# Joined attention maps transposed by DMA from SBUF to SBUF instead of by way of DRAM

## The chip, the cores and the metric

One Trainium2 chip; the kernel runs as one program on its 8 cores. The metric is the device time of the slowest core, in microseconds (us). Even cores and odd cores have different shares of the work (below), and so different spans.

## The reference, cut to what matters

One decoder block on x (4 x 4096 x 2048) with 16 meta tokens ahead of each sequence. Its input projection feeds two mixers, whose outputs are gated, added, projected and followed by a squared-ReLU MLP. The change lies in the first mixer, differential attention, with 4 heads:

```
s = einsum('bhcqd,bhckd->bhcqk', q, k) * scale      # two maps c = 0, 1
p = softmax(where(kpos <= qpos, s, -inf))           # per map
a = p[:, :, 0] - lam * p[:, :, 1]                   # the joined map
o = einsum('bhqk,bhkd->bhqd', a, v)                 # V has 256 columns
```

The last product contracts over keys, so TensorE needs the joined map with the keys on the partitions: it has to be transposed.

## The kernel before

**Tiling.** A sequence is shared by two cores. The even core ("a" in the tile names) has the first 18 blocks of 128 queries, the odd core ("b") the last 14, and each computes keys and values for all blocks that its queries see (19 on a, with the block of the meta tokens; 33 on b). The phases: 1 makes keys, values and queries; 2 runs attention and retention; 3 the gates and the merge; 4 the output projection; 5 the MLP.

**Phase 2** works on units: one head and one block of 128 queries, 72 units on core a and 56 on core b. Within a head the blocks run downwards in heads 0 and 2 and upwards in heads 1 and 3, so a unit's joined map is 128 x n with n from 256 to 2432 columns on a (2 to 19 blocks of 128 keys) and from 20 to 33 blocks on b. A unit passes through these steps, each a closure that `slot(u)` puts at a fraction of a slot:

- `qk(u, c, g)`: a matmul of up to 512 keys into one of three PSUM banks, then an exponential on ACT (L1284) into `P`. Map 0 goes to `P[u % 2]` (tiles `P_59` and `P_60`), map 1 to `P[2]` (`P_61`).
- `ratio(u)` and `join(u)` (L1308, on DVE), in slot u + 1: the joined map, written in place into `P[u % 2]`.
- `store_a(u)`, at 0.27 of slot u + 1: a DMA of the joined map to DRAM, into `A_d[u % 3]`.
- `load_a(u)`, at 0.62 of slot u + 1: a transposing DMA from `A_d` into `aT[u % LAG]` (tiles `aT_62` to `aT_64` on a); it waits until the store has landed.
- `av(u)`, in slot u + LAG: n / 128 matmuls of `aT` with `V`. LAG is 3 on core a and 2 on core b.

The matmuls of retention (`queue`, `pull`) are spread between these steps, as filling. Between the phases nothing waits for all engines; the first weights of phase 3 (`w_0_2`, `w_0_3` on core a) come in eight pieces each on POOL's DMA queue, each piece waiting for the one before on the same semaphore, and POOL works its stream in order: pieces, small statistics, and the add of `mo` (L1485) of phase 3.

**What sets the order.** Every operation is recorded once (`Prog.op`) with its dependences by buffer. `Prog.schedule` then plays a list schedule with a cost for each operation and writes one stream per engine in the order of that play; at run time each engine works its stream in order and waits on semaphores where a dependence crosses engines. All plain and transposing DMAs here are issued by SP (its queue is shown as SPq, all of its issues at L272, inside `Prog.dma`); loads of weights, which cast to bf16, are issued by POOL. A waiting DMA on SP so holds back all that SP issues behind it. TensorE's matmuls all have line L437, in the helper `mm`; they are told apart by their tiles.

**Buffers that matter.** `P[u % 2]` is read by the joining step and by the store; the exponentials of unit u + 2 overwrite it and so wait for the store's landing. `aT[u % LAG]` is overwritten by the transpose of unit u + LAG, which waits for `av(u)`. The tiles of phase 2 are put by `place`, first fit, into three free stretches of SBUF.

Of the kernel before, what the change touches and what calls it, by code (L numbers as in the profile page):

```python
# [9 lines left out]
BF16 = mybir.dt.bfloat16  # L10
# [363 lines left out]
class Core:  # L374
# [102 lines left out]
    def build(self):  # L477
        nc, p, io = self.nc, self.p, self.io
        self.PSA = io["ps"]
        self.PS = [io["ps"][:, 512 * i:512 * (i + 1)] for i in range(8)]  # L480
        self.PB = [p.buf("ps%d" % i) for i in range(8)]
        T, nch = self.T, self.nch
        self.KT_d = self.dram("KT_d", [4, 128, 2, T], BF16)
        self.V_d = self.dram("V_d", [128, 4, nch, 256], BF16)
        self.xnT_d = [self.dram("xnT%d_d" % i, [128, 16, 128 * n], BF16) for i, (c, n) in enumerate(self.tiles)]
        own = self.own_tiles
        self.QT_d = [self.dram("QT%d_d" % i, [4, 128, 2, 128 * n], BF16) for i, (c, n) in enumerate(own)]
        self.oa_d = self.dram("oa_d", [128 * self.nown, 1024], BF16)
        self.or_d = self.dram("or_d", [128 * self.nown, 1024], BF16)
        self.tT_d = [self.dram("tT%d_d" % i, [128, 16, 128 * n], BF16) for i, (c, n) in enumerate(own)]  # L490
        self.A_d = [self.dram("A%d_d" % i, [128, T], BF16) for i in range(3)]
        self.mT_d = [self.dram("mT%d_d" % i, [128, 16, 128 * n], BF16) for i, (c, n) in enumerate(own)]
        self.hnT_d = [self.dram("hnT%d_d" % i, [128, 16, 128 * n], BF16) for i, (c, n) in enumerate(self.mtiles)]
        self.h1_d = self.dram("h1_d", [self.nown * 128, D], F32)
        NT, NO = len(self.tiles), len(own)
        self.D_KT = [[p.buf("KT_d") for _ in range(NT)] for _ in range(4)]
        self.D_V = [p.buf("V_d") for _ in range(nch)]
        self.D_x = [p.buf("x_d") for _ in range(NT)]
        self.D_Q = [[p.buf("Q_d") for _ in range(NO)] for _ in range(4)]
        self.D_oa = [[p.buf("oa_d") for _ in range(4)] for _ in range(self.nown)]  # L500
        self.D_or = [[p.buf("or_d") for _ in range(4)] for _ in range(self.nown)]
        self.D_tT = [[p.buf("tT_d") for _ in range(2)] for _ in range(NO)]
        self.S_tT = [p.dsem("tT%d" % i) for i in range(2)]
        self.D_A = [p.buf("A_d") for _ in range(3)]
        self.D_m = [[p.buf("m_d") for _ in range(4)] for _ in range(NO)]
        self.D_h1 = [p.buf("h1_d") for _ in range(self.nown)]
        self.D_hn = [p.buf("hn_d") for _ in self.mtiles]

        off = 0
        cst, self.B_cst = self.sb("cst", [128, NCST], F32, off)  # L510
        off += -(-NCST * 4 // 64) * 64
        cstb, self.B_cstb = self.sb("cstb", [128, 256], BF16, off)
        off += 512
        gs4, self.B_gs4 = self.sb("gs4", [128, 256], F32, off)
        off += 1024
        small, self.B_small = self.sb("small", [128, 8], F32, off)
        off += 32
        negh, self.B_negh = self.sb("negh", [128, 4], F32, off)
        off += 32
        self.O = off  # L520
        assert self.base + off + 200 * KB <= self.limit
        self.cst = cst
        self.gs4 = gs4
        self.ident = cstb[:, 0:128]
        self.mask = cstb[:, 128:256]
        self.neglam = small[:, 4:5]
        self.S_c = p.dsem("c")
        S_cb = p.dsem("cb")
        S_nh = p.dsem("nh")
        self.small, self.negh = small, negh  # L530
        self.p1_weights()
        p.dve(lambda h: h.memset(small[:, 7:8], 0.0), writes=[self.B_small])
        p.act(lambda h: h.activation(out=small[:, 6:7], in_=small[:, 7:8], func=AF.Square), writes=[self.B_small])
        p.dma("sp", S_nh, [(negh[:], io["cst"][:, C_NH:C_NH + 4])], writes=[self.B_negh])
        p.dma("pool", S_cb, [(cstb[:], io["cb"][:, :])], writes=[self.B_cstb])
        self.phase1()
        self.phase2()
        self.phase3()
        self.phase4()
        self.phase5()  # L540
        p.emit()
# [324 lines left out]
    def phase2(self):  # L866
        p, io, O = self.p, self.io, self.O
        cst = self.cst
        PS, PB = self.PS, self.PB
# [18 lines left out]
        def mem(name, n, shape, dt, dma=False):  # L888
            size = -(-int(np.prod(shape[1:])) * (4 if dt == F32 else 2) // 32) * 32
            return self.ring(name, n, shape, dt, place(n * size), dma=dma)  # L890
# [11 lines left out]

        LAG = self.ng + 1
        P, B_P, _ = mem("P", 3, [128, T], BF16)
        aT, B_aT, S_aT = mem("aT", LAG, [128, nch, 128], BF16, True)
        tmp, B_tmp, _ = mem("tR", 6, [128, 384], F32)
        rkt, B_rkt, _ = mem("rkt", 2, [128, 3, 256], BF16)
        rvz, B_rvz, _ = mem("rvz", 2, [128, 3, 256], BF16)
# [13 lines left out]
        sm, B_sm, _ = mem("sm", 1, [128, 128], BF16)  # L922
        st3, B_st3, _ = mem("st3", 2, [128, 8], F32)
        onb, B_onb, S_onb = mem("onb", 2, [128, 256], BF16, True)
        S_A = [p.dsem("A%d" % i) for i in range(3)]
        if Z:
            for i in range(2):
                p.dve(lambda e, i=i: e.memset(P[i][:, 0:Z], 0.0), writes=[B_P[i]])
# [339 lines left out]
        def pbuf(u, c):  # L1268
            return 2 if c else u % 2
# [38 lines left out]
            p.dve(lambda e: e.scalar_tensor_tensor(out=P[a][:, k0:k1], in0=P[b][:, k0:k1], scalar=sta[st][:, 24:25], in1=P[a][:, k0:k1],  # L1308
                                                   op0=ALU.mult, op1=ALU.add), reads=[B_P[b], B_sta[st]], writes=[B_P[a]])

        def store_a(u):
            h, ch = units[u]
            n = 128 * (ch + 1)
            i = u % 3
            p.dma("sp", S_A[i], [(self.A_d[i][:, 0:n], P[pbuf(u, 0)][:, 0:n])], reads=[B_P[pbuf(u, 0)]], writes=[self.D_A[i]])

        def load_a(u):
            h, ch = units[u]
            n = 128 * (ch + 1)
            i = u % LAG  # L1320
            p.dma("sp", S_aT[i], [(aT[i][:, 0:ch + 1, :], self.A_d[u % 3][:, 0:n])], reads=[self.D_A[u % 3]], writes=[B_aT[i]], transpose=True)

        def av(u, b0, b1):
            h, ch = units[u]
            i = u % LAG
            for b in range(b0, b1):
                self.mm(PS[AV_][:, 0:256], [(aT[i][:, b, :], V[:, b, :])], [B_aT[i], B_V[b // 8]], [PB[AV_]], start=(b == 0), stop=(b == ch))
                if (b == ch or (b + 1) % 8 == 0) and last_use[h, b // 8] == u and h + 1 < 4:
                    load_V(h + 1, b // 8)
            if b1 == ch + 1:  # L1330
                st = u % (LAG + 2)
                k = u % 2
                p.dve(lambda e: e.tensor_scalar(out=o1[k][:], in0=PS[AV_][:, 0:256], scalar1=sta[st][:, 22:23], scalar2=None, op0=ALU.mult),
                      reads=[B_sta[st]], writes=[PB[AV_], B_o1[k]])
                p.act(lambda e: e.activation(out=oab[k][:], in_=o1[k][:], func=AF.Square, accum_out=sta[st][:, 26:27]),
                      reads=[B_o1[k]], writes=[B_oab[k], B_sta[st]])
                self.stat(sta[st], B_sta[st], 26, 1.0 / 256, EPS)
# [11 lines left out]
        def slot(u):  # L1349

            S = []
            if u < NU:
                h, ch = units[u]
                gs = [(c, g) for c in range(2) for g in range(len(ugroups[u]))]
                for i, (c, g) in enumerate(gs):
                    w = ugroups[u][g][1] + 75.0
                    S.append(((i + 0.5) / len(gs), w, lambda c=c, g=g: qk(u, c, g)))
                S.append((0.3, 0.0, lambda: load_Q(u + 2)))
            if 0 <= u - 1 < NU:
                n = 128 * (units[u - 1][1] + 1)  # L1360
                js = even(n - Z, 512)
                S.append((0.0, 0.0, lambda: ratio(u - 1)))
                for i, (k0, w) in enumerate(js):
                    S.append((0.01 + 0.25 * i / len(js), 0.0, lambda k0=k0, w=w: join(u - 1, Z + k0, Z + k0 + w)))
                S.append((0.27, 0.0, lambda: store_a(u - 1)))
                S.append((0.62, 0.0, lambda: load_a(u - 1)))
            if 0 <= u - LAG < NU:
                v = u - LAG
                nb = units[v][1] + 1
                bs = even(nb, 4)  # L1370
                first = 0.5 if v > 0 and units[v][0] != units[v - 1][0] else 0.15
                for i, (b0, m) in enumerate(bs):
                    w = 0.0 if u < NU else 150.0 * m
                    S.append((first + (0.98 - first) * (i + 0.5) / len(bs), w, lambda b0=b0, m=m: av(v, b0, b0 + m)))
            if 0 <= u - LAG - 1 < NU:
                S.append((0.1, 0.0, lambda: fin(u - LAG - 1)))
            S.sort(key=lambda t: t[0])
            return S
# [539 lines left out]
```

How the kernel before makes its waits and increments, by code:

```python
    def then_inc(self, *a):  # L63
        return self
# [203 lines left out]
        def fn(h):  # L268
            ins = None
            for (o_, i_) in pairs:
                start = h.dma_start_transpose if transpose else h.dma_start
                ins = start(out=o_, in_=i_).then_inc(h16, 16)
            return ins
# [19 lines left out]
    def _emit_stream(self, h, e, ops):  # L293
        waited = self.waited[e]
        for o in ops:
            need = {}
            for t in o.need:
                if t.is_dma:
                    key, g = ("d", id(t.sem)), t.val
                else:
                    key, g = ("e", t.eng), t.sigcount
                if waited.get(key, 0) >= g:
                    continue
                if key not in need or need[key][0] < g:
                    need[key] = (g, t)
            for key, (g, t) in need.items():
                waited[key] = g
                if t.is_dma:
                    h.wait_ge(t.sem.h, g)
                else:
                    h.wait_ge(self._engsem(t.eng, (g - 1) // EPOCH), (g - 1) % EPOCH + 1)
            ins = o.fn(h)
            if (not o.is_dma) and o.signal:
                g = o.sigcount
                ins.then_inc(self._engsem(e, (g - 1) // EPOCH), 1)
```

## Time and profile before

| | us |
|---|---|
| median of 3 runs | 4331.31 |
| lowest and highest | 4329.52, 4791.88 |
| the profiled execution | 4335.62 |
| span of its slowest core (core 2, an even one) | 4333.5 |
| span of core 3, its odd neighbour | 4233.6 |

The profiled execution lies 4.3 us over the median; its span lacks 2.1 us of its own time. On core 2 TensorE is busy for 4187.9 us (97%). Phase 2 lies between 478 and 1320 us on core 2, and between 662 and 1860 us on core 3. A span is from the first to the last instruction of a core; "granted clock" is the share of TensorE's full clock that it was given.

### The profile page before, as it was taken

How to read it: one execution, taken by the hardware profiler on the slowest of the kernel's cores; microseconds unless marked ns; L12 is line 12 of the kernel's file. 1: busy time of each engine (PE TensorE's matmuls, PEld its weight loads, DVE VectorE, ACT ScalarE, POOL GpSimd, SP SyncE). 2: the span in 40 equal slices, each digit the busy share in tenths (PEclk: the TensorE clock that was granted, in tenths of full speed). 3: DMA queues.
4: the chain of work that ended last, by engine and by line, in shares of the span. 5: the costliest groups of instructions: out<-in, count | busy, mean ns of one | idle time of the engine just before them, and what ended most of it. 6: DMA issues, size and time to landing. Idle time of an engine off the chain costs nothing.

```text
span 4333.5 us, 68916 instructions; the slowest of 8 cores (4225.0 to 4333.5 us)
## 1 busy us (share of the span) xinstructions
PE 4187.9 (97%) x24108; PEld 2315.1 (53%) x24108; DVE 1580.5 (36%) x2818; ACT 894.5 (21%) x2232; POOL 665.2 (15%) x1143
## 2 busy tenths in 40 slices
PE   5899998999988999999999999999999999999998
PEld 3455465555554666665445555555555555555554
DVE  4243477767751111111333333322235333222334
ACT  2111355655541111111122000011102000111002
POOL 3232222222222222222000000000001000000000
PEclk9999999999999999999999999999999999999999
DMA  7644788788778665666768444444449444444442
GB/s 201 143 134 111 159 179 189 156 192 190 164 169 192 171 164 138 162 151 168 231 198 251 90 69 68 67 66 68 69 75 270 79 69 68 68 68 68 68 68 97
DMA packets 368120, 574.84 MB, mean 133 GB/s; under 512 B 187296, under 2 KB 282144, under 8 KB 351904
## 3 DMA queue, kind: packets, MB, share of 16 engines
q0 software_dynamic: 77904, 197.23, 29.8%
q1 hardware_dynamic: 289872, 373.15, 29.3%
q8 instruction: 200, 3.28, 0.3%
q14 instruction: 144, 1.18, 0.1%
HBM read 608.37 MB, written 124.91 MB: 169 GB/s over the span
## 4 chain that ended last, share of the span: by engine, by line
PE 88%; DMA 6%; SPq 2%; issue 1%; DVE 1%; ACT 1%; POOL 1%; DVEq 0%; POOLq 0%; ACTq 0%
PE ps L437 87%; SPq L272 2%; DMA A_d_a<-sb_a_P_59_119 1%; DMA A_d_a<-sb_a_P_60_120 1%; PE ps L467 1%; DMA V_d_a<-sb_a_vs_41_101 1%; DMA sb_a_xR_50_110<-xnT_d_a 1%; DMA sb_a_xf_14_74<-xin 1%; DMA sb_a_w_0_2_114_174<-w 0%; DMA sb_a_aT_63_123<-A_d_a 0%; DMA sb_a_g_12_72<-gb 0%; DMA sb_a_KT_52_112<-KT_d_a 0%; DMA sb_a_aT_64_124<-A_d_a 0%; DMA sb_a_xR_53_113<-xnT_d_a 0%; DMA mT_d_a<-sb_a_mo_125_185 0%
## 5 line engine op out<-in xcount | busy, mean ns | idle before, releaser
L1713 ACT ACTIVATE sb_a_rl_166_226<-ps 128x384 f32<-128x384 f32 x192 | 94.4, 492 | 1275.8 <-PE ps L437 1275.8
L1713 ACT ACTIVATE sb_a_rl_167_227<-ps 128x384 f32<-128x384 f32 x192 | 94.5, 492 | 395.2 <-PE ps L437 390.7
L437 PE MATMUL ps<-sb_a_wR_109,sb_a_xR_50_110 128*128 128x512 bf16 x608 | 152.8, 382 | 0.0
L437 PE MATMUL ps<-sb_a_xR_50_110,sb_a_wR_109 128*128 128x384 bf16 x768 | 148.6, 329 | 3.9 <-DMA sb_a_xR_50_110<-xnT_d_a 3.0
L437 PE MATMUL ps<-sb_a_wR_109,sb_a_xR_53_113 128*128 128x512 bf16 x608 | 152.2, 379 | 0.0
L437 PE MATMUL ps<-sb_a_xR_53_113,sb_a_wR_109 128*128 128x384 bf16 x768 | 146.7, 328 | 0.9 <-DVE sb_a_tR_66_126 L1050 0.9
L1284 ACT ACTIVATE sb_a_P_61_121<-ps 128x464 bf16<-128x464 f32 (+15 forms) x216 | 110.2, 510 | 123.3 <-PE ps L437 97.8
L437 PEld LDWEIGHTS ps<-sb_a_xR_50_110,sb_a_wR_109 128*128 128x128 bf16 x768 | 73.3, 99 | 47.6 <-issue 6.8
L437 PEld LDWEIGHTS ps<-sb_a_xR_53_113,sb_a_wR_109 128*128 128x128 bf16 x768 | 73.4, 98 | 44.8 <-issue 3.4
L1482 DVE SCALAR_TENSOR_TENSOR sb_a_m_120_180<-sb_a_tg_116_176,ps 128x384 f32<-128x384 f32 x48 | 26.6, 555 | 188.7 <-PE ps L437 115.2
L1482 DVE SCALAR_TENSOR_TENSOR sb_a_m_123_183<-sb_a_tg_119_179,ps 128x384 f32<-128x384 f32 x48 | 26.6, 554 | 174.6 <-ACT sb_a_tg_119_179 L1480 174.6
L437 PEld LDWEIGHTS ps<-sb_a_wR_109,sb_a_xR_50_110 128*128 128x128 bf16 x608 | 57.8, 98 | 54.1 <-issue 1.4
L437 PEld LDWEIGHTS ps<-sb_a_wR_109,sb_a_xR_53_113 128*128 128x128 bf16 x608 | 57.4, 98 | 54.0
L1482 DVE SCALAR_TENSOR_TENSOR sb_a_m_121_181<-sb_a_tg_117_177,ps 128x384 f32<-128x384 f32 x48 | 26.6, 553 | 160.4 <-ACT sb_a_tg_117_177 L1480 159.9
L1482 DVE SCALAR_TENSOR_TENSOR sb_a_m_122_182<-sb_a_tg_118_178,ps 128x384 f32<-128x384 f32 x48 | 26.6, 555 | 135.1 <-PE ps L437 98.7
L1480 ACT ACTIVATE sb_a_tg_119_179<-ps 128x384 f32<-128x384 f32 x48 | 23.6, 491 | 225.7 <-PE ps L437 225.7
L1480 ACT ACTIVATE sb_a_tg_117_177<-ps 128x384 f32<-128x384 f32 x48 | 23.6, 491 | 224.9 <-PE ps L437 220.2
L1738 DVE TENSOR_TENSOR sb_a_acc_181_241<-ps,sb_a_acc_181_241 128x512 f32<-128x512 f32 x64 | 44.3, 691 | 62.5 <-PE ps L437 62.3
L1738 DVE TENSOR_TENSOR sb_a_acc_180_240<-ps,sb_a_acc_180_240 128x512 f32<-128x512 f32 x64 | 44.2, 691 | 62.3 <-PE ps L437 62.1
L1738 DVE TENSOR_TENSOR sb_a_acc_182_242<-ps,sb_a_acc_182_242 128x512 f32<-128x512 f32 x64 | 44.3, 691 | 60.9 <-PE ps L437 60.7
L1738 DVE TENSOR_TENSOR sb_a_acc_183_243<-ps,sb_a_acc_183_243 128x512 f32<-128x512 f32 x64 | 44.2, 691 | 60.9 <-PE ps L437 60.7
L1738 DVE TENSOR_TENSOR sb_a_acc_185_245<-ps,sb_a_acc_185_245 128x512 f32<-128x512 f32 x64 | 44.2, 691 | 60.1 <-PE ps L437 59.5
(706 smaller groups left out, 9412.2 us busy)
## 6 DMA issues: line engine op xcount, KB each, us to landing
sb_a_xR_53_113<-xnT_d_a SPq DMA_DIRECT2D x24, 768.0 KB, 6.0
sb_a_xR_50_110<-xnT_d_a SPq DMA_DIRECT2D x24, 768.0 KB, 6.4
sb_a_x_0_111_171<-xnT_d_a SPq DMA_DIRECT2D x24, 768.0 KB, 6.4
sb_a_x_1_126_186<-xnT_d_a SPq DMA_DIRECT2D x24, 768.0 KB, 6.9
sb_a_wb_151_211<-w_up POOLq DMA_DIRECT2D x22, 512.0 KB, 5.9
sb_a_wb_152_212<-w_up POOLq DMA_DIRECT2D x22, 512.0 KB, 5.7
sb_a_wb_153_213<-w_up POOLq DMA_DIRECT2D x22, 512.0 KB, 5.6
sb_a_wb_155_215<-w_up POOLq DMA_DIRECT2D x22, 512.0 KB, 5.9
```

Source lines behind the costliest of these rows:

```text
L272: ins = start(out=o_, in_=i_).then_inc(h16, 16)
L437: ins = h.matmul(out_ap, l, r, start=(start and i == 0), stop=(stop and i == n - 1), skip_group_check=loose)
L467: ins = h.transpose(pv[:, k * 128:(k + 1) * 128], xn[:, kc * 128:(kc + 1) * 128], self.ident)
L1284: p.act(lambda e: e.activation(out=P[b][:, k0:k0 + w], in_=PS[bk][:, 0:w], func=AF.Exp, scale=scale, accum_out=sta[st][:, 10 * c + g:10 * ...
L1480: p.act(lambda e, q=q, gb=gb, n=n, bs=bs, f2=f2: e.activation(out=tg[f2 + q][:, 0:n], in_=PS[bs + gb][:, 0:n], func=AF.Tanh, scale=0.5), w ...
L1482: p.dve(lambda e, q=q, yb=yb, n=n, bs=bs, f2=f2: e.scalar_tensor_tensor(out=m12[f2 + q][:, 0:n], in0=tg[f2 + q][:, 0:n], scalar=1.0, in1=P ...
L1713: p.act(lambda e, r=r, bk=bk, n=n: e.activation(out=rl[r][:, 0:n], in_=PS[bk][:, 0:n], func=AF.Relu), writes=[PB[bk], B_rl[r]])
L1738: p.dve(lambda e: e.tensor_tensor(out=acc[m][:, nsl], in0=PS[bk][:], in1=acc[m][:, nsl], op=ALU.add), writes=[PB[bk], B_acc[m]])
```

## The change

`store_a` and `load_a` become one step, `turn`, at 0.27 of slot u + 1, where `store_a` stood: a transposing DMA from `P[u % 2]` in SBUF to `aT[u % LAG]`. The buffers in DRAM and their semaphores go. Each `aT` tile becomes a flat row of 128 x nch elements with 112 elements (224 bytes) behind it.

```diff
-        self.A_d = [self.dram("A%d_d" % i, [128, T], BF16) for i in range(3)]
-        self.D_A = [p.buf("A_d") for _ in range(3)]
-        aT, B_aT, S_aT = mem("aT", LAG, [128, nch, 128], BF16, True)
+        aT, B_aT, S_aT = mem("aT", LAG, [128, 128 * nch + 112], BF16, True)
-        S_A = [p.dsem("A%d" % i) for i in range(3)]
-        def store_a(u):
-            h, ch = units[u]
-            n = 128 * (ch + 1)
-            i = u % 3
-            p.dma("sp", S_A[i], [(self.A_d[i][:, 0:n], P[pbuf(u, 0)][:, 0:n])], reads=[B_P[pbuf(u, 0)]], writes=[self.D_A[i]])
-        def load_a(u):
+        def turn(u):
             h, ch = units[u]
             n = 128 * (ch + 1)
             i = u % LAG
-            p.dma("sp", S_aT[i], [(aT[i][:, 0:ch + 1, :], self.A_d[u % 3][:, 0:n])], reads=[self.D_A[u % 3]], writes=[B_aT[i]], transpose=True)
+            p.dma("sp", S_aT[i], [(aT[i][:, 0:n].rearrange("p (b q) -> p b q", q=128), P[pbuf(u, 0)][:, 0:n])], reads=[B_P[pbuf(u, 0)]], writes=[B_aT[i]], transpose=True)
-                self.mm(PS[AV_][:, 0:256], [(aT[i][:, b, :], V[:, b, :])], [B_aT[i], B_V[b // 8]], [PB[AV_]], start=(b == 0), stop=(b == ch))
+                self.mm(PS[AV_][:, 0:256], [(aT[i][:, 128 * b:128 * (b + 1)], V[:, b, :])], [B_aT[i], B_V[b // 8]], [PB[AV_]], start=(b == 0), stop=(b == ch))
-                S.append((0.27, 0.0, lambda: store_a(u - 1)))
-                S.append((0.62, 0.0, lambda: load_a(u - 1)))
+                S.append((0.27, 0.0, lambda: turn(u - 1)))
```

## Rows read from the trace of the kernel before

**Rows 1.** Cores: span and mean granted clock.
```profile
core 2: 4333.5 us, clock 0.988
core 3: 4233.6 us, clock 0.982
```

**Rows 2.** Windows, cores 2 and 3: PE, PEld, DVE, ACT, POOL busy; clock, DMA share, GB/s.
```profile
478.00:1320.00 842.00, 773.39 (x4827) 452.66 (x4825) 550.20 (x1288) 443.10 (x1472) 195.88 (x417) 0.97 0.80 178
...
662.00:1860.00 1198.00, 1085.46 (x6483) 623.76 (x6481) 696.11 (x1557) 673.40 (x2114) 166.10 (x347) 0.96 0.83 198
```

**Rows 3.** Waits of PE, core 2, 495 to 1320: us in total, times, longest.
```profile
PE ps L437 <- DMA sb_a_w_0_2_114_174<-w: 17.3, 1, 17.3
PE ps L437 <- DMA sb_a_aT_64_124<-A_d_a: 12.3, 2, 9.7
PE ps L437 <- ACT sb_a_P_59_119 L1284: 7.2, 4, 3.3
...
PE ps L437 <- DMA sb_a_aT_62_122<-A_d_a: 2.5, 3, 1.5
PE ps L437 <- ACT sb_a_P_60_120 L1284: 2.0, 2, 1.2
```

**Rows 4.** Waits of ACT, core 2, 478 to 1320.
```profile
ACT sb_a_P_60_120 L1284 <- DMA A_d_a<-sb_a_P_60_120: 17.8, 10, 3.5
...
ACT sb_a_P_59_119 L1284 <- DMA A_d_a<-sb_a_P_59_119: 12.3, 7, 3.4
```

**Rows 5.** Waits of SP's queue, core 2, 478 to 1320.
```profile
SPq L309 <- DMA A_d_a<-sb_a_P_60_120: 64.6, 26, 8.2
SPq L309 <- DMA A_d_a<-sb_a_P_59_119: 51.5, 21, 7.1
```

**Rows 6.** Timeline, core 2, units 0 and 69: store, transpose, the buffer's next exponential.
```profile
495.44 0.34 SPq L272 DMA_DIRECT2D A_d_a<-sb_a_P_59_119  x1
498.42 3.33 SPq L272 DMA_TRANSPOSE sb_a_aT_62_122<-A_d_a  x1
...
522.37 0.52 ACT L1284 ACTIVATE sb_a_P_59_119<-ps 128x413 bf16<-128x413 f32 x1 [0.91 <-PE ps L437]
...
1242.32 0.33 SPq L272 DMA_DIRECT2D A_d_a<-sb_a_P_60_120  x1
...
1245.25 2.38 SPq L272 DMA_TRANSPOSE sb_a_aT_62_122<-A_d_a  x1
...
1252.93 0.55 ACT L1284 ACTIVATE sb_a_P_60_120<-ps 128x464 bf16<-128x464 f32 x1
```

**Rows 7.** Tile aT, core 2: single transposes of 2 and of 19 blocks, issue and landing.
```profile
L272 SPq DMA_TRANSPOSE sb_a_aT_62_122<-A_d_a x1: 1212/1212/1212, 1094.9 to 1094.9; - x1
...
DMA to landing us min/median/max: 2.9/2.9/2.9
...
L272 SPq DMA_TRANSPOSE sb_a_aT_64_124<-A_d_a x1: 2943/2943/2943, 886.2 to 886.2; - x1
...
DMA to landing us min/median/max: 5.0/5.0/5.0
```

**Rows 8.** Timeline, core 2, end of phase 2: SP's queue, PE and POOL.
```profile
1273.11 0.33 SPq L272 DMA_DIRECT2D A_d_a<-sb_a_P_60_120  x1
1281.73 4.43 SPq L272 DMA_TRANSPOSE sb_a_aT_64_124<-A_d_a  x1
...
1291.40 4.21 PE L437 MATMUL ps<-sb_a_V_118,sb_a_aT_64_124 128*128 128x256 bf16 x19 [9.72 <-DMA sb_a_aT_64_124<-A_d_a]
...
1318.28 2.08 PE L437 MATMUL ps<-sb_a_x_0_111_171,sb_a_w_0_2_114_174 128*128 128x384 bf16 x6 [17.27 <-DMA sb_a_w_0_2_114_174<-w]
...
1288.77 0.60 POOL L272 DMA_DIRECT2D sb_a_w_0_2_114_174<-w  x1 [4.33 <-DMA sb_a_w_0_2_114_174<-w]
...
1303.35 0.62 POOL L272 DMA_DIRECT2D sb_a_w_0_2_114_174<-w  x1
```

**Rows 9.** DMA queue of SP, core 2, 1320 to 2340: packets, MB, share of 16 engines.
```profile
q1 hardware_dynamic: 58323, 148.89, 44.9%
```

## The prediction

> **What bounds the kernel now.** I read the cores first: core 2 ends the run at 4333.5 us, its odd neighbour core 3 ends 99.9 us earlier [rows 1]. So whatever the change does to odd cores is free until it costs them 100 us, and nothing gained there counts. Next the windows: in phase 2, the only one that the change touches, TensorE of core 2 is busy for 773.4 of 842 us at a granted clock of 0.97, and DMA is busy for 0.80 of the time [rows 2]. The phase is TensorE's, with 68.6 us of gaps to win at most. Then who ends those gaps: the weights `w_0_2` once for 17.3 us, the transposed maps for 12.3 and 2.5 us, exponentials into `P_59` and `P_60` for 7.2 and 2.0 us [rows 3]. Two waits of other engines belong to the store: ACT stood 30.1 us in 17 waits for a store to land before it could overwrite `P` [rows 4], and SP's queue 116.1 us in 47 waits before it could issue the transpose [rows 5]. Of ACT's 30.1 us, TensorE felt at most 9.2: a share of 0.31, which I use below as the price of a wait of ACT.
>
> **The change part by part.** *The store goes.* On core 2 that is 72 issues of 0.33 us, 756 blocks of 128 x 128 bf16 (4 heads, 2 to 19 blocks), 24.8 MB. Its DMA time isn't in the trace by itself; in the next phase plain transfers dominate SP's DMA queue, and there 148.89 MB took 44.9% of 1020 us, 3.08 us per MB [rows 9]: some 76 us of busy DMA, so that the share of phase 2 falls from 0.80 to about 0.71, if a transpose costs what it did. I count nothing for the relief: TensorE's waits are latencies of single transfers (a loss is excluded, a gain is kept for the range).
>
> *SP's wait goes.* The transpose is issued where the store was. In unit 0 that is 495.44 instead of 498.42, in unit 69 1242.32 instead of 1245.25 [rows 6]; and at the end of the phase 1273.11 instead of 1281.73 [rows 8]. What stands behind it on SP (loads of `xR`, `QT`, K and V, stores of outputs) moves up by the 1.6 us a unit that the 116.1 us come to, less what the longer transposes hold SP.
>
> *The end of the phase.* The last transpose comes 8.6 us earlier. Now it lands at 1291.1, TensorE multiplies by V from 1291.40 (9.72 us of gap), then does a group of phase 3 whose result POOL adds, and only behind that does POOL issue the seventh piece of `w_0_2` at 1303.35; two pieces later TensorE goes on at 1318.28 [rows 8]. The sixth was issued at 1288.77, and the last two took 14.9 us for their two landings, 7.5 each, so the seventh can't go before 1296.3: 7.1 of the 8.6 us come through. Gain 7.1 us.
>
> *The waits for aT earlier in the phase.* They are 2.6 us (12.3 less the 9.7 at the end) and 2.5 us [rows 3], all in units of few blocks, where slots are short. A map that comes as much earlier as SP waited makes them vanish. Gain 5.1 us.
>
> *P is held longer.* This is the cost. The exponential of unit u + 2 waits for whoever reads `P[u % 2]` last. For the first 70 units I took its start less the landing of the store: 24.0 us in unit 0, 7.8 in unit 69 (the first and last of the 70 [rows 6]), 3.2 on average, under 0.3 in 21 units, where ACT waited. Now I put the transpose in the store's place, with its own landing (6.8 us in unit 0, 6.0 in unit 69): the average falls to 1.7 us, 21 units are below zero, by 35 us in all. At 0.31 that is 10.9 us lost. Behind the waiting exponential ACT holds evictions of retention and of the gates, so TensorE can feel more than the share says when both of their banks are full; behind it in turn is all of the filling.
>
> *The price of a transpose that reads SBUF* is not in the trace. The nearest row is the transpose out of DRAM: 2.9 us to landing for 2 blocks and 5.0 for 19, so 0.12 us a block on top of 2.7; it holds SP for 1.21 and 2.94 us, 0.10 a block [rows 7]. The destination and the crossing are the same and only the source moves, so I take the same price. Below, I bound it by the store's landing in its place (no buffer held longer, the 10.9 us not lost); above, by 0.52 a block, four times the row, where the queues fill (rivals). With x us more a block, the time that the 70 units lack grows from 35 us to 44 (x = 0.05), 73 (0.15) and 138 us (0.30).
>
> The Trainium skill has a price for this: "DMA: Bandwidth & Descriptors", section on why a DMA increments its semaphore by 16, table of sequencer times, gives older generations 262,144 cycles for 8,192 tiles from SBUF, one push each, against 512 cycles for a plain copy. A plain issue is 0.33 us here [rows 8], so 32 cycles would be 21 ns, and with eight tiles of 16 rows a block 0.17 us: an estimate, 0.05 above the row. By it the sum would be 2.8 us worse, and the slow rival less likely.
>
> *The 224 bytes and the order.* Three `aT` tiles grow by 672 bytes a partition together, so `rkt` no longer fits in the first free stretch and lies elsewhere; nothing of it is on the path at the start of the phase, 0 us (bounds 0 to 3). The planner plays the new graph, with its own cost for a transpose, and may reorder fillings: 0 with 8 us either way. The matmul of `av` reads the same columns by another index: 0.
>
> *Sum.* 4335.6 - 7.1 - 5.1 + 10.9 = 4334.3 for an execution like the profiled one; it lay 4.3 us over the median, so **4330 us**, 1 us under before: no change. What is late next on core 2 is the exponential behind the held `P`, and at the end the chain of `w_0_2` pieces.
>
> *Odd cores.* Their units have 20 to 33 blocks and slots of 21 us (1198 us, 56 units [rows 2]); the same count for 54 units gives 6.2 us on average before, 3.1 after, 30 us lacking: 9 us of their 99.9.
>
> **The rivals.** *A: reading SBUF makes the transpose dear, and the kernel slower.* Place: phase 2 of the odd cores, which move 1484 blocks (4 heads, 20 to 33) and whose DMA is busy for 0.83 of 1198 us already, 994 us [rows 2]. The store takes 48.6 MB x 3.08 = 150 of it away, leaving 844; x more a block adds 1484 x. From x = 0.31 the phase is DMA's and longer by 100 us, and core 3 is the last core; from 0.36 the kernel is over 2% slower. At x = 0.40 it is 1438 us, 240 longer: 4233.6 + 240 - 2.2 = 4471. For it: a share of 0.83 has little room, and SP would be held longer too. Against: the row's 0.12 would have to grow more than threefold.
>
> *B: somewhat dearer.* At x = 0.15 the lacking time is 73 us, 38 more, at 0.31 another 12: 4342. For it: sources lie row by row in single partitions, where DRAM had them anywhere. In the Trainium skill this is a rule: "SBUF — State Buffer", Door 1, the port swizzle, lets 16 neighbouring partitions reach 4 of the 16 ports at 27.2 GB/s; an estimate from it is 0.30 us a block, and no row here shows it.
>
> *C: the latencies fall.* If the lighter DMA queue and the near source bring the landing down to the store's, the 10.9 us of loss stay out, and of rows 3 the waits for aT before the end, for `P` (9.2) and for `w_0_2` go: 4335.6 - 17.3 - 9.7 - 5.1 - 9.2 - 4.3 = 4290. For it: 116 us less standing on SP. Against: `w_0_2` is a chain of eight landings, which only partly shortens.
>
> *D: the round trip was hidden.* If a delayed exponential costs nothing because three PSUM banks cover it, only the gains stay: 4330 - 11 = 4319. Inside the likeliest range.
>
> **How the numbers follow.** The sum (with D) 0.61, its own range 4308 to 4348; B 0.17; A 0.14; C 0.06; the change not doing what it says, with TensorE waiting in `av` for maps that are late as before, 0.02 (4331). The range reaches up into A as far as its start, and down to C: 4295 to 4420. A measurement of this kernel can tell about 2% from no change, that is 87 us: faster than that needs more than all of the phase's gaps, 0.02; slower is A without its low end, 0.13; within 0.85.
>
> **What would show it.** Right: no DMA writes to `A_d`; SP's waits for it gone; the last `av` of phase 2 some 7 us earlier and `w_0_2` with it; ACT's waits for `P` now on the transpose, some 50 to 70 us in all; landings of transposes near 3 us for 2 blocks and 5 to 7 for 19. Wrong: a transpose of 19 blocks that lands after 10 us or more, DMA's share in phase 2 above 0.9, or core 3 as the last core.

## The result and the profile after

| | before | after |
|---|---|---|
| median, us | 4331.31 (3 runs); 4333.11 (4 runs beside the changed kernel) | 4310.58 |
| ratio after to before, 95% interval | | 0.9949, 0.9926 to 0.9971 |
| measured once more (e9), ratio | | 0.9947, 0.9933 to 0.9961 |
| span of core 2 in the profile, us | 4333.5 | 4305.9 |
| span of core 3, us | 4233.6 | 4175.6 |

The change gains about 0.5%, some 22 us: less than the 2% from which on a kernel counts as faster here, but the interval stays under 1. Ratios, intervals and ranges here leave out the runs in which one half of the chip had a lower granted clock.

Cores and windows of the changed kernel, beside [rows 1, 2] (the columns are the same):

```profile
core 2: 4305.9 us, clock 0.988
core 3: 4175.6 us, clock 0.984
```

```profile
478.00:1320.00 842.00, 796.72 (x4978) 469.35 (x4977) 552.99 (x1294) 447.69 (x1478) 201.26 (x427) 0.97 0.71 152
...
662.00:1860.00 1198.00, 1131.88 (x6836) 657.72 (x6833) 704.33 (x1572) 677.96 (x2129) 185.99 (x374) 0.97 0.76 167
```

The window of 842 us now holds 23.3 us more of TensorE's work on core 2; DMA's share falls from 0.80 to 0.71. The odd core's span shrinks twice as much as core 2's, by 58.0 us against 27.6, but that doesn't show in the time: even cores still end the run.

Waits of PE (core 2, 495 to 1320), beside [rows 3], then those of ACT for `P`, beside [rows 4]:

```profile
PE ps L437 <- DMA sb_a_w_0_2_114_174<-w: 16.9, 1, 16.9
PE ps L437 <- DMA sb_a_aT_64_124<-sb_a_P_60_120: 3.2, 1, 3.2
PE ps L437 <- DMA sb_a_aT_62_122<-sb_a_P_59_119: 2.7, 2, 2.0
...
PE ps L437 <- ACT sb_a_P_59_119 L1281: 1.1, 1, 1.1
```

```profile
ACT sb_a_P_59_119 L1281 <- DMA sb_a_aT_63_123<-sb_a_P_59_119: 8.6, 2, 7.3
...
ACT sb_a_P_59_119 L1281 <- DMA sb_a_aT_64_124<-sb_a_P_59_119: 4.7, 2, 2.8
ACT sb_a_P_60_120 L1281 <- DMA sb_a_aT_63_123<-sb_a_P_60_120: 4.4, 3, 1.8
...
ACT sb_a_P_59_119 L1281 <- DMA sb_a_aT_62_122<-sb_a_P_59_119: 4.2, 3, 3.2
```

Here is the first surprise: ACT waits 21.9 us for `P` (the four rows), not the 50 to 70 of the forecast, and less than the 30.1 of [rows 4], although `P` is now held through the whole transpose. It is hardly held longer: SP issues the transpose 0.22 us behind the last joining instruction, where the store came 0.67 us behind it, and `P` is free 5.09 us behind that instruction instead of 4.90 (means over the 72 units of core 2).

SP's queue: of the 116.1 us that it stood for `A_d` [rows 5] nothing is left; it stands in front of later work instead (the first of these rows was 71.4 us before):

```profile
SPq L311 <- PE ps L437: 155.2, 57, 26.5
SPq L311 <- DVE sb_a_P_60_120 L1305: 49.9, 22, 5.5
```

The end of phase 2, beside [rows 8]: the last transpose, its `av`, the seventh piece of `w_0_2`, and the matmul that waited for the eighth.

```profile
1257.25 3.45 SPq L272 DMA_TRANSPOSE sb_a_aT_64_124<-sb_a_P_60_120  x1
...
1265.02 4.21 PE L437 MATMUL ps<-sb_a_V_118,sb_a_aT_64_124 128*128 128x256 bf16 x19 [3.19 <-DMA sb_a_aT_64_124<-sb_a_P_60_120]
...
1278.21 0.54 POOL L272 DMA_DIRECT2D sb_a_w_0_2_114_174<-w  x1
...
1292.17 4.32 PE L437 MATMUL ps<-sb_a_x_0_111_171,sb_a_w_0_2_114_174 128*128 128x384 bf16 x13 [16.86 <-DMA sb_a_w_0_2_114_174<-w]
```

The `w_0_2` matmul comes 26.1 us earlier (1318.28 to 1292.17). I use its start as the mark of how far phase 2 has come. The first of the eight pieces was issued at 1252.52 before and at 1236.23 after: 16.3 of the 26.1 us are won ahead of the tail, 9.8 in it.

One transpose of 19 blocks, unit 0, from the view of its tile (6.8 us to landing before, issued at 498.42 [rows 6]):

```profile
L272 SPq DMA_TRANSPOSE sb_a_aT_62_122<-sb_a_P_59_119 x1: 2844/2844/2844, 493.9 to 493.9; - x1
...
DMA to landing us min/median/max: 4.8/4.8/4.8
```

Over all 72 transposes of core 2 the mean landing fell from 5.82 to 4.87 us; that of the store that stood in this place was 4.23.

### The profile page after: what moved, and what is told of

The parts are those of the page before. It is cut to its first block, busy times and chain, and to the rows that moved or that the text cites. A ratio compares the mean times of both kernels' runs of the same rounds, so it can differ in the third digit from the quotient of the medians.

```text
span 4305.9 us, 68790 instructions; the slowest of 8 cores (4157.2 to 4305.9 us)
## 1 busy us (share of the span) xinstructions
PE 4184.4 (97%) x24108; PEld 2315.9 (54%) x24108; DVE 1581.1 (37%) x2818; ACT 895.3 (21%) x2232; POOL 665.5 (15%) x1143
## 4 chain that ended last, share of the span: by engine, by line
PE 92%; DMA 4%; SPq 2%; issue 1%; DVE 1%; ACT 1%; POOL 1%; POOLq 0%; DVEq 0%; ACTq 0%
PE ps L437 91%; SPq L272 2%; PE ps L467 1%; DMA sb_a_xf_14_74<-xin 1%; DMA V_d_a<-sb_a_vs_41_101 0%; DMA sb_a_w_0_2_114_174<-w 0%; DMA sb_a_xR_53_113<-xnT_d_a 0%; DMA sb_a_aT_64_124<-sb_a_P_60_120 0%; DMA sb_a_g_12_72<-gb 0%; DMA sb_a_aT_62_122<-sb_a_P_59_119 0%; DMA sb_a_aT_63_123<-sb_a_P_59_119 0%; DMA mT_d_a<-sb_a_mo_125_185 0%; DMA sb_a_wb_151_211<-w_up 0%; DMA sb_a_xR_50_110<-xnT_d_a 0%; PE ps L1091 0%
## 5 line engine op out<-in xcount | busy, mean ns | idle before, releaser
L437 PEld LDWEIGHTS ps<-sb_a_wR_109,sb_a_xR_50_110 128*128 128x128 bf16 x608 | 57.3, 98 | 52.4
L1729 DVE TENSOR_TENSOR sb_a_acc_180_240<-ps,sb_a_acc_180_240 128x512 f32<-128x512 f32 x64 | 44.3, 692 | 62.3 <-PE ps L437 62.1
L1281 ACT ACTIVATE sb_a_P_59_119<-ps 128x464 bf16<-128x464 f32 (+18 forms) x108 | 55.0, 509 | 57.5 <-PE ps L437 35.2
L1729 DVE TENSOR_TENSOR sb_a_acc_182_242<-ps,sb_a_acc_182_242 128x512 f32<-128x512 f32 x64 | 44.3, 692 | 61.3 <-PE ps L437 61.1
L1729 DVE TENSOR_TENSOR sb_a_acc_183_243<-ps,sb_a_acc_183_243 128x512 f32<-128x512 f32 x64 | 44.3, 692 | 61.2 <-PE ps L437 61.0
L1729 DVE TENSOR_TENSOR sb_a_acc_181_241<-ps,sb_a_acc_181_241 128x512 f32<-128x512 f32 x64 | 44.3, 692 | 61.1 <-PE ps L437 60.9
```

The costliest lines, as they stand in the source:

```text
L437: ins = h.matmul(out_ap, l, r, start=(start and i == 0), stop=(stop and i == n - 1), skip_group_check=loose)
L1281: p.act(lambda e: e.activation(out=P[b][:, k0:k0 + w], in_=PS[bk][:, 0:w], func=AF.Exp, scale=scale, accum_out=sta[st][:, 10 * c + g:10 * ...
L1729: p.dve(lambda e: e.tensor_tensor(out=acc[m][:, nsl], in0=PS[bk][:], in1=acc[m][:, nsl], op=ALU.add), writes=[PB[bk], B_acc[m]])
```

## The experiments

Where the gain comes from is read from a ladder between the two kernels: e1 (and e10) take away the round trip alone, e12 and e2 the bytes too, and the changed kernel adds the planner's new order. In the cuts of code, "..." stands for lines left out.

**e1 and e10: the wait goes, the bytes stay.** The planner plays the graph of before; then, in the streams that it wrote, the store becomes the transpose from SBUF, and the old transpose becomes a DMA of the store's size that nobody reads. The orders of PE, DVE, ACT and POOL are those of before, to the instruction.

```diff
         self.schedule()
...
+        for k, tr in enumerate(self.trips):
+            st, ld = tr[0], tr[-1]
...
+            st.fn, st.sem, st.val, ld.sem, ld.val = ld.fn, ld.sem, ld.val, st.sem, st.val
...
+            ld.fn = tr[1]
...
+            p.trips.append([o, lambda h: h.dma_start(out=d32, in_=c32).then_inc(S_A[i].h, 16), self.B_cst.w])
...
```

> The order of every engine is that of the kernel before, to the instruction. Where the store was issued, SP issues the transpose from SBUF; where the old transpose stood, it issues a plain DMA of the old size from a constant tile to DRAM that nobody waits for. So the 24.8 MB are still written on core 2, but no transpose waits for them. Theory 1 (the wait itself): the gain of the changed kernel comes from the map that lands some 6 us earlier and from SP that no longer stands; then this kernel has most of it, 4333 - 15 to 20, ratio 0.995 to 0.997. Theory 2 (relief): the gain comes from the bytes that no longer load the DMA queues; then nothing is gained here, ratio 1.000, or up to 1.003 if P is held longer. Theory 3 (the planner's new order): ratio 1.000 to 1.003 too, and the next kernel the same.

Measured: 4320.52 and 4325.05 us, where before ran at 4325.81 to 4334.47 (seven runs) and 4351.41. Two runs give no interval; e10 is the same kernel:

> e1 once more, for an interval, since only two of its runs could be used (4320.52 and 4325.05). If the ladder so far holds (8 us from the wait that goes, 11 us from the bytes that go, 2 us from the new order), it comes to 4320 to 4325, ratio 0.9975 to 0.9985. If the bytes are nothing and only e1's few runs were high, 4312, ratio 0.9955; if the wait is nothing, 4331, ratio 1.000.

Measured: 0.9988, 0.9969 to 1.0008 (nine runs, eight at 4325.57 to 4333.50 and one at 4343.53). The wait by itself, with whatever the longer holding of `P` costs, is worth 5 us, and not surely different from nothing; by e1's two runs it is some 9 (the median of before beside them is 4332.2).

**e2: the bytes go too.** As e1, with the old transpose taken out of SP's stream.

```diff
-            ld.fn = tr[1]
...
+            self.streams["sp"].remove(ld)
...
```

> As the kernel before in every engine's order, but with the transpose from SBUF in the store's place and nothing in the place of the old transpose: the change without the planner's new order. Theory 1 (the wait itself): the same as the kernel with the dummy writes, within 3 us. Theory 2 (relief): 15 to 22 us faster than the kernel before and than the kernel with dummy writes, ratio 0.995 to 0.9965. Theory 3 (the new order): ratio 1.000 to 1.003, and only the full change shows the 22 us.

Measured: 0.9944, 0.9922 to 0.9965 (4308.71 to 4314.93). That is all of the gain of the full change, with the order of before. The step from e10, measured on another chip, is 0.0044 of 4331, 19 us, and the two intervals just don't meet; from e1's two runs, on the same chip, it is 11.

**e12: the issues stay, the bytes go.** In e2 72 issues on SP go together with the bytes. Here the dummy DMA stays but writes 8 partitions:

```diff
-            d32, c32 = self.A32_d[i][:, 0:n // 2], cst[:, 0:m]
+            d32, c32 = self.A32_d[i][0:8, 0:n // 2], cst[0:8, 0:m]
...
```

> As e10, but each dummy DMA writes 8 partitions instead of 128: the 72 issues on SP's queue stay on core 2, the bytes fall from 24.8 MB to 1.5 MB and the packets with them. If e10 lies above e2 because the DMA queues carry the bytes, this comes down to e2: 4313, ratio 0.9945 to 0.9955. If it is the 72 issues and SP's time for them, it stays with e10: ratio 0.998 to 0.9995.

Measured: 4308.94 and 4313.10 us (two runs, no interval; before ran at 4327.42 to 4339.23 beside them), as e2 and below every run of e10. So it is what the queues carry, not the number of issues. SP's DMA queue (packets, MB, share of 16 engines) and the median landing of the transposes, core 2, 478 to 1320, of e10 and of e12:

```profile
q1 hardware_dynamic: 186582, 129.11, 61.7%
...
sb_a_aT<-sb_a_P SPq DMA_TRANSPOSE x72, 4.6
```

```profile
q1 hardware_dynamic: 183936, 109.11, 53.8%
...
sb_a_aT<-sb_a_P SPq DMA_TRANSPOSE x72, 4.5
```

The transposes hardly feel the bytes. Others feel them more: from e10 to e2 the median landing of `xR` falls from 6.0 to 5.3 us, that of `QT` from 3.9 to 3.4, that of the weights `w` from 5.0 to 4.5 (transposes 4.6 to 4.4). PE's waits for DMA, core 2, 478 to 1320, of e10 and of e2:

```profile
PE ps L459 <- DMA sb_a_w<-w: 20.1, 1, 20.1
...
PE ps L459 <- DMA sb_a_xR<-xnT_d_a: 5.8, 2, 3.6
PE ps L459 <- DMA sb_a_x<-xnT_d_a: 4.6, 1, 4.6
```

```profile
PE ps L457 <- DMA sb_a_w<-w: 13.7, 1, 13.7
PE ps L457 <- DMA sb_a_x<-xnT_d_a: 4.5, 1, 4.5
PE ps L457 <- DMA sb_a_xR<-xnT_d_a: 2.6, 1, 2.6
```

All rows of that view, grouped by what ended the wait (us, core 2, 478 to 1320), and the mark of the end of the phase:

| | before | e10 | e12 | e2 | after |
|---|---|---|---|---|---|
| weights `w_0_2` | 17.3 | 20.1 | 13.7 | 13.7 | 16.9 |
| `aT` | 16.4 | 1.5 | 0 | 0 | 11.0 |
| other loads | 7.4 | 13.4 | 7.8 | 9.3 | 3.8 |
| exponentials into `P` | 15.7 | 14.9 | 13.5 | 14.0 | 7.3 |
| all, with the rest | 67.2 | 57.0 | 44.0 | 45.3 | 44.2 |
| first `w_0_2` matmul at | 1318.28 | 1308.48 | 1285.07 | 1290.91 | 1292.17 |

Read from before to e10 and on to e2: the round trip's end takes 14.9 us of waits for `aT` away, but while the bytes are still there the loads of `x`, `xR`, `QT` and weights are waited for longer instead, by 8.8 us. Without the bytes these waits fall by 10.5. On the mean of the four even cores, TensorE's waits for weights and other loads are 26.2 us before, 33.6 in e10, 25.4 in e12 and 23.2 in e2. So before and e2 differ little in them: in the waits, the net gain is that of `aT` (14.7 us before and none in e2, on that mean), and it is kept only once the bytes are gone too. The planner's new order then trades waits for `P` and for loads (12.2 us less) against waits for `aT` and `w_0_2` (14.2 more): nothing beyond the noise, as the times say too (0.9944 and 0.9949).

**e5: the transpose at its old place.** As e2, but the store is taken out of SP's stream, and the transpose from SBUF stays where the transpose stood. `P` is held longer; the orders of the other engines are those of e2.

```diff
-            self.streams["sp"].remove(ld)
+            self.streams["sp"].remove(st)
+            ld.deps = [t for t in ld.deps + st.deps if t is not st]
...
```

> As e2 (every other engine in the order of before, no store, transpose from SBUF), but SP issues the transpose where the old transpose stood, not where the store stood. P is so held some 10 us behind the joining step instead of 5, and the map lands as much later. By the trace of before 57 of 70 exponentials of core 2 would then be late, by 187 us in all. If a wait of ACT costs TensorE the share of my prediction (0.31), the kernel is 58 us slower than e2: about 4370, ratio 1.009. If TensorE's work and the PSUM banks cover it and only the DMA traffic counted, it stays within 5 us of e2: ratio 0.994 to 0.996.

Measured: 1.0149, 1.0115 to 1.0184 (4400.44 to 4402.63), slower than either forecast. On core 2, ACT's waits for `P` by transposes and PE's for exponentials (both 478 to 1320), and the window 495 to 1236 (PE; clock, DMA share, GB/s):

```profile
ACT sb_a_P L1298 <- DMA sb_a_aT<-sb_a_P: 120.2, 36, 8.3
```

```profile
PE ps L451 <- ACT sb_a_P L1298: 64.4, 29, 7.6
```

```profile
495.00:1236.00 741.00, 658.24 (x4024) 0.95 0.62 131
```

The first and the last of these for e2:

```profile
ACT sb_a_P L1304 <- DMA sb_a_aT<-sb_a_P: 18.5, 11, 3.6
```

```profile
495.00:1236.00 741.00, 721.65 (x4568) 1.00 0.69 147
```

ACT's waits grow by 101.7 us and the kernel by 88 (4400.5 against 4312): 0.87 us of time for each us, not 0.31. PE's waits for exponentials explain 50 of the 88 (14.0 to 64.4). A matmul costs 163.6 ns of busy time here and 158.0 in e2 (busy time by count), some 26 us over 4568 of them: TensorE stands more in this window, the granted clock is lower (0.95 against 1.00), and its work takes longer as well.

**e3: P held through both landings, and the planner knows.** The store comes back, the transpose waits for it, but reads `P`.

```diff
-                S.append((0.27, 0.0, lambda: turn(u - 1)))
+                S.append((0.27, 0.0, lambda: store_a(u - 1)))
+                S.append((0.62, 0.0, lambda: turn(u - 1)))
-            p.dma("sp", S_aT[i], [(aT[i][:, 0:n].rearrange("p (b q) -> p b q", q=128), P[pbuf(u, 0)][:, 0:n])], reads=[B_P[pbuf(u, 0)]], writes=[B_aT[i]], transpose=True)
+            p.dma("sp", S_aT[i], [(aT[i][:, 0:n].rearrange("p (b q) -> p b q", q=128), P[pbuf(u, 0)][:, 0:n])], reads=[B_P[pbuf(u, 0)], self.D_A[u % 3]], writes=[B_aT[i]], transpose=True)
+        def store_a(u):
...
```

> The store to DRAM comes back and the transpose waits for its landing as before, but reads P in SBUF, so P is held through both landings. On the trace of before this makes 61 of 70 exponentials of core 2 late, by 244 us in all. By the share of my prediction (0.31 us of TensorE for each us of ACT's wait) that costs 76 us: about 4407, ratio 1.017. If the three PSUM banks and the planner's order cover the wait (the holding is nearly free), the ratio stays under 1.005. If ACT's wait reaches TensorE whole, about 4570, ratio 1.055.

Measured: 4333.51 and 4336.98 us (two runs, no interval), 1 and 5 us over the median of before on the same chip, 4332.2. Of the three forecasts, "nearly free" came true. Waits of ACT (478 to 1320) and of PE (same window), core 2:

```profile
ACT sb_a_P L1284 <- DMA sb_a_aT<-sb_a_P: 73.4, 38, 8.5
```

```profile
PE ps L437 <- DMA sb_a_aT<-sb_a_P: 20.9, 12, 9.8
...
PE ps L437 <- ACT sb_a_P L1284: 9.4, 16, 1.7
```

ACT waits 73.4 us here, over twice as long as before, and PE's waits for exponentials are no longer than before: 9.4 us. The planner had played the held buffer, and its order is another than that of before; that this order covers the wait is the likeliest reason, since e5 kept the old order and paid, but no run tests it alone. The static count of 244 us was three times too high as well; in e5, in the order of before, 187 were counted and 120.2 measured. The reason may be that a late exponential moves everything behind it, so that the next one isn't late by its full lack again; this wasn't tested.

**e6: a third buffer for map 0** (even cores only, where it fits).

```diff
-        P, B_P, _ = mem("P", 3, [128, T], BF16)
+        P, B_P, _ = mem("P", 3 + (self.ng == 2), [128, T], BF16)
...
-            return 2 if c else u % 2
+            return 1 + self.ng if c else u % (1 + self.ng)
```

> The changed kernel with three buffers for map 0 on the even cores instead of two, so that no exponential waits for a transpose. If the holding of P costs what my prediction said, this gains what is left of it: ACT's 21.9 us of waits on core 2 vanish, 7 us at 0.31: about 4303, ratio 0.993 to 0.9935. If those waits are covered, ratio 0.995, as the changed kernel.

Measured: 0.9953, 0.9907 to 0.9998. The ratio shows no gain over the changed kernel, though none of ACT's waits ends at a transpose any more; PE waits longer for the weights (18.1 us, once). The interval is wide because of one run at 4352.66. The other five lie at 4304.90 to 4308.93, where e7, the changed kernel but for its spare bytes, ran at 4307.90 to 4315.49 on the same chip: a gain of some 6 us is not excluded.

**e7: no spare bytes.**

```diff
-        aT, B_aT, S_aT = mem("aT", LAG, [128, 128 * nch + 112], BF16, True)
+        aT, B_aT, S_aT = mem("aT", LAG, [128, 128 * nch], BF16, True)
```

> The changed kernel without the 112 spare elements behind each destination; every engine has the same order. If the spare bytes matter (a destination row that ends on a shared boundary, another place of rkt), transposes land later and the ratio rises to 0.997 or more; if not, 0.995 and landings as in the changed kernel (mean 4.9 us on core 2).

Measured: 0.9944, 0.9922 to 0.9966; the median landing on core 2 is 4.4 us, as in e2. No effect of the 224 bytes is seen.

**e4 and e8: the weights at the end.** In e4 `p3_prefetch` issues the eight pieces of `w_0_2` as one operation, and so those of `w_0_3`; e8 does so for `w_0_2` alone, and `w_0_3` goes in four operations of two pieces.

```diff
-            self.p3_load_w(0, fb)
...
+            self.p.dma("pool", self.S_w3[fb % 2], [(t[:, 6 * i:6 * i + 6], self.io["w3"][0, fb, :, 6 * i:6 * i + 6]) for i in range(8)], writes=[b])
```

> The changed kernel, with the eight pieces of w_0_2, and those of w_0_3, issued as one operation of eight DMAs each, so that no piece waits for the one before. In the changed kernel TensorE waits 16.9 us for w_0_2 at the end of phase 2 on core 2. If that wait is the chain of eight landings, it vanishes and the kernel is 10 to 17 us faster than the changed one: about 4296, ratio to the kernel before 0.991 to 0.9925. If the transfers are limited by the bandwidth at that place (DMA busy for 0.94 of these 56 us), or the eight issues hold up POOL's adds, the ratio stays at 0.995.

Measured: 0.9924, 0.9887 to 0.9961 (4297.54, 4299.54, 4304.32). From three runs, the interval still holds the changed kernel's 0.9949; e11 below tells them apart. The wait for `w_0_2` is gone, but a new one has come. Timeline of core 2, SP and PE:

```profile
1240.85 11.88 SPq L272 DMA_TRANSPOSE sb_a_aT<-sb_a_P  x1
...
1260.55 4.00 PE L437 MATMUL ps<-sb_a_V,sb_a_aT 128*128 128x256 bf16 x18 [12.56 <-DMA sb_a_aT<-sb_a_P]
```

In the changed kernel the same transpose held SP for 4.66 us. Here POOL issued 16 pieces of weights, 3.1 MB, between 1235.06 and 1246.36, and the weights now stand in its way.

> As e4, but only w_0_2 is issued as eight DMAs at once; w_0_3 comes in four operations of two, each behind the one before. In e4 the wait for w_0_2 went, but 3.1 MB of weights were queued within 12 us just where the last but one transpose was issued: its issue took 11.88 us on core 2 instead of 4.66 and TensorE waited 12.6 us for it. If that is the cause, the transpose is back at 5 to 7 us and the kernel gains another 4 to 8 us: 4292 to 4297, ratio 0.991 to 0.992. If w_0_2 alone is enough to hold the transpose up, or w_0_3 is late, 4300 as e4, ratio 0.993.

Measured: 0.9926, 0.9898 to 0.9954 (4303.40 to 4306.25). The transpose still holds SP for 8.39 us, TensorE waits 5.2 us for it, and 7.6 us for the first transposing load of phase 3, which probably meets the rest of the weights (not tested). Spreading the burst gains nothing over e4.

**e9 and e11: the best version beside the changed kernel, on one chip.** e11 is e4 with e6's third buffer.

> The changed kernel once more, on the chip of the next two, so that they can be set against it directly: about 4310, ratio 0.995.

> e4's weights at once together with e6's third buffer on the even cores. If the third buffer gained nothing alone because whatever it gained was waited for again at the chain of w_0_2 (18.1 us of wait in e6 instead of 16.9), the two together beat e4 by 2 to 4 us: 4295 to 4298, ratio 0.991 to 0.9925. If ACT's waits for P were covered, the same as e4, 4300, ratio 0.993.

Measured: e9 0.9947, 0.9933 to 0.9961 (4307.59 to 4317.13); e11 0.9924, 0.9908 to 0.9940 (4298.10, 4300.10, 4303.46), each run of e11 under each run of e9. It beats both kernels, by some 11 us the changed one, and has the ratio of e4: the weights bring the gain, and nothing of the buffer shows beside them.

## Why the prediction was right, and where it was wrong

4330 us (no change by 2%, 4295 to 4420) against 4310.6: inside the range and within 2% of before, as forecast, but 19 us under the time forecast; two terms of the sum were wrong, both to the slow side. That the verdict of no change held is owed in part to the smallness of all the terms: the larger part of the gain came by a way that the sum had at nothing. By its own steps:

- *The store goes.* Right in size: SP's queue on core 2 gave back 61.7 - 52.4 = 9.3% of 842 us, 78 us (forecast 76), and the share of phase 2 is 0.71, as forecast. **The step that failed is the sentence behind it: "I count nothing for the relief".** I argued that TensorE's waits are latencies of single transfers. They are, but the latency of a load of `x`, `xR` or weights depends on what else the queues carry: the step from e10 to e2, with e12 as its control, is worth 11 to 19 us, once the wait is gone.
- *SP's wait goes.* It did, and by itself, with the earlier map, it is worth 5 to 9 us (e10, e1), against the 12.2 us that I had as the end of the phase and the waits for `aT`. The waits for `aT` vanished (16.4 to 1.5 us), but the waits for the loads beside them grew.
- *The end of the phase.* Forecast 7.1 us, measured 9.8 behind the first piece of `w_0_2`. The mechanism is that of the rows: piece seven comes behind the last `av` and a group of phase 3, and the wait of 17 us stays.
- *P is held longer, +10.9.* **The second step that failed; its sign.** I put the landings of before in the store's place (mean 5.82); the transpose out of SBUF landed after 4.87, only 0.64 later than the store's 4.23, and SP, which no longer stands, issues it 0.45 us sooner behind the joining step, so that `P` is held for 0.19 us more a unit. ACT's waits went from 30.1 to 21.9 us, and to 18.5 in e2, where the order is that of before. The two factors were wrong as well: the lack counted on a still trace is too high (e5: 187 counted, 120.2 measured), and the price of 0.31 is too low in e5, where the order doesn't know of the wait (0.87), and too high in e3, where it does (at most 5 us of time for 43 us more of ACT's wait than before, 0.1).
- *The price of a transpose that reads SBUF.* A line through the 72 landings of core 2 gives 3.58 us and 0.12 us a block after (3.26 and 0.14 in e9), 3.73 and 0.20 before: the 0.12 of the quiet rows stood. The source in SBUF is not dearer: in e10, which still carries the bytes, the mean landing is 5.14 us against 5.82. Single landings scatter more than I wrote, 2.3 to 5.4 us for 2 blocks and 4.8 to 8.6 for 19. So rivals A and B fell. The estimate of 0.30 us a block from the Trainium skill ("SBUF — State Buffer", Door 1) isn't seen either: the measurement decides.
- *The 224 bytes and the order*: 0 was right for both within the noise (e7; e2 against the changed kernel).
- *Odd cores.* I had them lose 9 us; they gained 58.0 (core 3). Their DMA was the busier (0.83, now 0.76), which may have been the hint.
- *Rivals D and C.* D, the sum without the loss on `P`, gave 4319; 11 us of relief off that is 4308, and 4310.6 was measured. C (latencies fall, 4290) had the right direction and half the size: other loads landed earlier, but the chain of `w_0_2` kept its 17 us.

What stays open: how the 22 us divide between wait and bytes is known to some 8 us only, since e1 and e10 differ by that; the division holds for this order of steps, since no run takes the bytes away and leaves the wait; the dummy writes of e10 come a little later in SP's stream than the store did; and those of e12 hold SP a little shorter than those of e10 (26.7 us in all against 35.9).

## What to carry to other kernels

When a transfer is taken away, price the transfers that stay: list the waits for any DMA in the stage, and give the relief a term of its own where the DMA share is as high as here (0.8). A wait of a side engine has no fixed price (0.87 in e5, at most 0.1 in e3): ask whether the order was planned with it. And a chain of small DMAs on one semaphore at a phase's end costs its landings in a row, but issued at once they can block the DMA that TensorE needs first.

## What the runs showed of the hardware

- A transpose and a burst of weights get in each other's way at the issue too: SP was held 11.88 us (e4) and 8.39 us (e8) by one DMA of 18 blocks that held it 4.66 us in the changed kernel.
- TensorE pays for this wait twice. Windows of 10 us around the wait for `w_0_2` in the changed kernel (PE busy; granted clock, DMA, GB/s):

```profile
1280.00:1290.00 10.00, 0.00 (x0) 0.50 1.05 298
1290.00:1300.00 10.00, 7.83 (x31) 0.59 0.43 60
1300.00:1310.00 10.00, 10.00 (x63) 1.00 0.61 71
```

While it stands the granted clock falls to 0.50 (1.2 GHz), and the first matmuls behind the wait take 253 ns each (7.83 us by 31) instead of 159 ns: another 2.9 us on 31 of them.
